# The inverse root of nine normalisations: ScalarE root and VectorE reciprocal, or one power instruction on GpSimd

## The chip, the core and the metric

The kernel runs on one core of a Trainium2 chip. The core's engines that matter here are TensorE (PE, matmuls; PEld is its weight load), VectorE (DVE), ScalarE (ACT), GpSimd (POOL) and SyncE (SP, which only issues loads). The metric is the device time of one execution in microseconds, lower is better; a kernel's figure is the median of its runs.

## What is computed

The program is two transformer-like blocks on one sequence of 256 tokens of width 1024. The first block has two layers, each with a projection, attention beside a Fourier mixer, an output projection and a gated feed-forward part; the second block has a feed-forward part, a mixer, and a second feed-forward part, with gains and shifts computed from a vector `c` by a large product `c_act @ w_ada`. Between these parts stand nine normalisations over the 1024 features:

```python
def layer_norm(x, g, b):                       # normalisations 0 to 4
    mu = jnp.mean(x32, axis=-1, keepdims=True)
    var = jnp.mean(jnp.square(x32 - mu), axis=-1, keepdims=True)
    return ((x32 - mu) * lax.rsqrt(var + LN_EPS) * g + b).astype(x.dtype)

def rmsnorm(x, g):                             # normalisations 5 to 8
    inv = lax.rsqrt(jnp.mean(xf * xf, axis=-1, keepdims=True) + EPS)
    return (xf * inv).astype(x.dtype) * g

def first_block(x, ...):
    h = layer_norm(x, ln_in_g, ln_in_b)                                    # 0
    for l in range(DEPTH):                                                 # DEPTH = 2
        ...
        h = layer_norm(ALPHA * h + mix, ln1_g[l], ln1_b[l])                # 1, 3
        h = layer_norm(ALPHA * h + swiglu(h, w_gu[l], w_down[l]), ...)     # 2, 4

def second_block(x, c, ...):
    u = modulate(rmsnorm(h, norm1_g[l]), mod[:, 0, 0], mod[:, 0, 1])       # 5
    h = h + FFN_RES_WEIGHT * ... * swiglu_2(u, ...)
    u = modulate(rmsnorm(h, norm2_g[l]), ...)                              # 6
    y = mixer(u, ...)
    u = modulate(rmsnorm(h, norm3_g[l]), ...)                              # 7
    ...
    return rmsnorm(h, final_g)                                             # 8
```

## The kernel before

**Layout.** Everything is kept transposed: features lie on the 128 partitions, in eight tiles `k`, and the 256 tokens lie along the row. `state[:, k, 0, :]` is the residual stream and `state[:, k, 1, :]` a scratch beside it. The weights come as 184 chunks of 128x2048 floats, `raw`, in three rotating buffers. Each chunk is split in two parts for an exact product: ACT rounds it to `w_hi` (L670) and DVE takes the rest as `w_lo` (L937). The activations are split in the same way, into `x_hi` (ACT, L696) and `x_lo` (DVE, L979), and every product is three matmuls (L335).

**Order.** There is no scheduler. Each engine has its own program, written out by hand, and the engines meet only at counting semaphores, so an engine that waits holds back all that stands behind it in its own program.

**One normalisation.** Both engines add up values and squares of the eight tiles (L1011, L1003). PE sums them over the partitions with two matmuls against a constant matrix (L388, L391), so that the mean and the mean square of each token stand on all 128 partitions, a tile of 128x256. DVE makes `var` of it: four steps for a layer norm (L946 to L953), one for an RMS norm (L944). The last of these raises `var_ready`. Then come the steps that the change touches:

- ACT waits for `var_ready` and takes the root, `rstd <- var` (L693; L927 for the last normalisation), and raises `std_ready`.
- DVE meanwhile subtracts the mean from tiles 0 and 1 in a layer norm (L960), then waits for `std_ready` and takes the reciprocal, `rstd <- rstd` (L967; L1391 for the last), and raises `rstd_ready`.
- DVE then scales the eight tiles one by one (L973). Each scaled tile goes to ACT for `x_hi`, and back to DVE for `x_lo`, and that raises `x_ready`, for which PE waits before it multiplies the tile. In the last normalisation the scaled tiles (L1394) are the output, which SP stores.

The instruction between `std_ready` and `rstd_ready`:

```python
                dve.wait_ge(std_ready, n + 1)
                nc.vector.reciprocal(rstd[:, :], rstd[:, :]).then_inc(rstd_ready, 1)
                dve.wait_ge(rstd_ready, n + 1)
```

**What PE does meanwhile.** After normalisations 2, 4 and 6 PE has `sum_ada` (L434), 48 small matmuls that add up a third of `c_act @ w_ada`; they wait for none of the normalisation's results. Behind normalisation 4 comes normalisation 5 at once, with nothing between but the squares. After the others PE has nothing until the first `x_lo`.

**GpSimd.** Its program loads two tables and then the 24 tiles of `w_ada` (1.5 MB each) into one buffer. Tile `a` is loaded when DVE has used up tile `a - 1`, which it does in the inner steps of three of the four feed-forward parts, eight tiles in each (L1064, L1067). Before the change it computes nothing.

**Tables of ScalarE.** Before an ACT instruction whose function is not in the active set, the build puts an ACT_TABLE_LOAD. Root, exponential, logarithm, sigmoid and the gate's Silu make it change; squares, copies and additions of a bias do not.

Of the kernel before, what the change touches and what calls it, by code (L numbers as in the profile page):

```python
# [27 lines left out]
ALU = mybir.AluOpType  # L28
ACT = mybir.ActivationFunctionType
AX_X = mybir.AxisListType.X  # L30

P = 128
S = 256
D = 1024
KT = D // P
DEPTH = 2
# [13 lines left out]
ADA_TILES = 9 * D // ADA_COLS  # L50
ADA_STEPS = FT - 3
# [22 lines left out]
def fused_blocks(nc, xT, stream, ada, w_f, layer_params, common_params, consts32, consts16, outT):  # L74
    with ExitStack() as ctx:
        def sb(name, shape, dt=F32):
            return ctx.enter_context(nc.sbuf_tensor(name, shape, dt))

        def sem(name):
            return ctx.enter_context(nc.semaphore(name))  # L80
# [19 lines left out]
        mean = sb("mean", [P, S])  # L100
        var = sb("var", [P, S])
        rstd = sb("rstd", [P, S])
        small = sb("small", [P, 128])
        partial = sb("partial", [P, 2, S])
        partial_last = sb("partial_last", [P, 2, S])
# [93 lines left out]
        mean2_ready = sem("mean2_ready")  # L199
        var_raw = sem("var_raw")  # L200
        var_ready = sem("var_ready")
        std_ready = sem("std_ready")
        rstd_ready = sem("rstd_ready")
        centered = sem("centered")
        scaled = sem("scaled")
# [76 lines left out]
        @block.sync  # L282
        def _(sp):
            for j in range(4):
                sp.dma_start(state[:, 2 * j:2 * j + 2, 0, :],
                             xT[2 * j * P:(2 * j + 2) * P, :].rearrange("(k p) n -> p k n", p=P))\
                  .then_inc(x_landed[j], 16)

            for s in range(SLOTS):
                sp.dma_start(raw[s][:, :], stream[s]).then_inc(raw_landed[s], 16)  # L290
                if s == 1:
                    sp.dma_start(c32[:, 0:ONES_D], consts32[:, 0:ONES_D]).then_inc(consts_landed, 16)
                    sp.dma_start(c32[:, TRI:], consts32[:, TRI:]).then_inc(consts_landed, 16)
            with sp.Fori(1, N_CHUNKS // SLOTS) as t:
                for s in range(SLOTS):

                    sp.wait_ge(lo_ready, 3 * t + (s - 2))
                    sp.dma_start(raw[s][:, :], stream[bass.ds(3 * t + s, 1)].rearrange("a p n -> (a p) n"))\
                      .then_inc(raw_landed[s], 16)
            for c in range(N_CHUNKS // SLOTS * SLOTS, N_CHUNKS):  # L300
                sp.wait_ge(lo_ready, c - 2)
                sp.dma_start(raw[c % SLOTS][:, :], stream[c]).then_inc(raw_landed[c % SLOTS], 16)
            for j in range(4):
                sp.wait_ge(out_ready, 2 * j + 2)
                sp.dma_start(outT[2 * j * P:(2 * j + 2) * P, :].rearrange("(k p) n -> p k n", p=P),
                             state[:, 2 * j:2 * j + 2, 1, :]).then_inc(stored, 16)
            sp.wait_ge(stored, 64)
# [4 lines left out]
        @block.gpsimd  # L312
        def _(pool):
            pool.dma_start(cp[:, :], common_params).then_inc(common_landed, 16)
            pool.wait_ge(raw_landed[1], 16)
            pool.dma_start(c16[:, :], consts16).then_inc(alibi_landed, 16)
            pool.dma_start(ada_raw, ada[0]).then_inc(ada_landed, 16)
            with pool.Fori(1, ADA_TILES) as a:

                pool.wait_ge(ada_step, KT * a)  # L320
                pool.dma_start(ada_raw, ada[bass.ds(a, 1)].rearrange("a p k n -> (a p) k n")).then_inc(ada_landed, 16)

# [339 lines left out]
        def _(act):  # L664
# [7 lines left out]
            def squares(n, j, ready):  # L672
                ready(j)
                nc.scalar.activation(state[:, 2 * j:2 * j + 2, 1, :], state[:, 2 * j:2 * j + 2, 0, :], ACT.Square)\
                    .then_inc(squares_done, 1)
# [11 lines left out]
            def after_residual(m):  # L687
                return lambda j: act.wait_ge(resid_done, 4 * m + (j + 1))

            def norm(n, shift, full):  # L690

                act.wait_ge(var_ready, n + 1)
                nc.scalar.activation(rstd[:, :], var[:, :], ACT.Sqrt).then_inc(std_ready, 1)  # L693
                for k in range(KT):
                    act.wait_ge(scaled, 8 * n + (k + 1))
                    nc.scalar.activation(x_hi[:, k, :], state[:, k, 1, :], ACT.Identity, bias=shift(k))\  # L696
                        .then_inc(x_hi_ready, 1)
                    if full:
                        nc.scalar.activation(state[:, k, 0, :], state[:, k, 1, :], ACT.Identity, bias=shift(k))\
                            .then_inc(full_ready, 1)  # L700
# [45 lines left out]
            split(0, 0, first=True)  # L746
            split(0, 1, first=True)
            norm(0, lambda k: cp[:, LNI_B + k:LNI_B + k + 1], True)

            with act.Fori(0, DEPTH) as l:  # L750
# [69 lines left out]
                for m in range(2):  # L820
# [3 lines left out]
                                         scale=subg).then_inc(mix_a_hi, 1)  # L824
                squares_of_pairs(2 * l + 1, 2 * l, t, O0)
                norm(2 * l + 1, lambda k: lp[:, LN1_B + k:LN1_B + k + 1], True)
                split(t, O0 + 6)
                ffn(t, G0, l)
                for j in range(4):
                    squares(2 * l + 2, j, after_residual(2 * l + 1))  # L830
                split(t, LAYER_CHUNKS + 1)
                norm(2 * l + 2, lambda k: lp[:, LN2_B + k:LN2_B + k + 1], True)


# [88 lines left out]
            ffn(MIX_T, MIX_CHUNKS, 3, final=True)  # L923
            for j in range(4):
                squares(8, j, after_residual(6))
            act.wait_ge(var_ready, 9)
            nc.scalar.activation(rstd[:, :], var[:, :], ACT.Sqrt).then_inc(std_ready, 1)  # L927

# [2 lines left out]
        def _(dve):  # L933
# [6 lines left out]
            def norm_stats(n, eps, rms):  # L940

                dve.wait_ge(stats_done, n + 1)
                if rms:
                    nc.vector.tensor_scalar(var[:, :], STATS[:, S:2 * S], eps, None, ALU.add).then_inc(var_ready, 1)  # L944
                else:
                    nc.vector.tensor_copy(mean[:, :], STATS[:, 0:S]).then_inc(mean_ready, 1)  # L946
                    dve.wait_ge(mean_ready, n + 1)
                    nc.vector.scalar_tensor_tensor(var[:, :], mean[:, :], -1.0, mean[:, :], ALU.mult, ALU.mult)\
                        .then_inc(mean2_ready, 1)
                    dve.wait_ge(mean2_ready, n + 1)  # L950
                    nc.vector.tensor_tensor(var[:, :], STATS[:, S:2 * S], var[:, :], ALU.add).then_inc(var_raw, 1)
                    dve.wait_ge(var_raw, n + 1)
                    nc.vector.tensor_scalar(var[:, :], var[:, :], 0.0, eps, ALU.max, ALU.add).then_inc(var_ready, 1)  # L953

            def norm(n, gain, shift, rms):

                norm_stats(n, RMS_EPS if rms else LN_EPS, rms)

                def center(k):
                    nc.vector.tensor_tensor(state[:, k, 1, :], state[:, k, 0, :], mean[:, :], ALU.subtract)\  # L960
                        .then_inc(centered, 1)

                if not rms:
                    center(0)
                    center(1)
                dve.wait_ge(std_ready, n + 1)
                nc.vector.reciprocal(rstd[:, :], rstd[:, :]).then_inc(rstd_ready, 1)  # L967
                dve.wait_ge(rstd_ready, n + 1)
                for k in range(KT + 1):
                    if k < KT:  # L970
                        if not rms:
                            dve.wait_ge(centered, 8 * n + (k + 1))
                        nc.vector.scalar_tensor_tensor(state[:, k, 1, :], state[:, k, 0 if rms else 1, :], gain(k),  # L973
                                                       rstd[:, :], ALU.mult, ALU.mult).then_inc(scaled, 1)
                        if not rms and k + 2 < KT:
                            center(k + 2)
                    if k >= 1:
                        dve.wait_ge(x_hi_ready, 8 * n + k)
                        nc.vector.scalar_tensor_tensor(x_lo[:, k - 1, :], state[:, k - 1, 1, :], shift(k - 1),  # L979
                                                       x_hi[:, k - 1, :].bitcast(F32), ALU.add, ALU.subtract)\  # L980
                            .then_inc(x_ready, 1)
# [405 lines left out]


            norm_stats(8, RMS_EPS, True)
            dve.wait_ge(std_ready, 9)  # L1390
            nc.vector.reciprocal(rstd[:, :], rstd[:, :]).then_inc(rstd_ready, 1)  # L1391
            dve.wait_ge(rstd_ready, 9)
            for k in range(KT):
                nc.vector.scalar_tensor_tensor(state[:, k, 1, :], state[:, k, 0, :],  # L1394
# [108 lines left out]
```

## Time and profile before

| | |
|---|---|
| median of 3 runs | 1327.15 us (1324.51 to 1329.25) |
| span of the profiled execution | 1327.0 us |
| TensorE matmul busy | 1239.0 us, 93% |
| TensorE weight load busy | 1183.8 us, 89% |
| VectorE busy | 857.9 us, 65% |
| ScalarE busy | 589.8 us, 44% |
| GpSimd busy | 14.1 us, 1% |
| chain that ended last | PE 86%, DVE 6%, ACT 4%, issue 3%, DMA 1% |

The span runs from the first to the last instruction. The busy shares say that PE is the engine to wait for in most of the program. They are averages over stages, though: what matters for a change in the normalisations is where PE stands still, and what it waits for there. The list of waits and the order in time (the timeline) tell that; in both, the bracket or the last columns name the idle time of an engine just before an instruction and the instruction that ended it.

### The profile page before, as it was taken

How to read it: one execution, taken by the hardware profiler on the slowest of the kernel's cores; microseconds unless marked ns; L12 is line 12 of the kernel's file. 1: busy time of each engine (PE TensorE's matmuls, PEld its weight loads, DVE VectorE, ACT ScalarE, POOL GpSimd, SP SyncE). 2: the span in 40 equal slices, each digit the busy share in tenths (PEclk: the TensorE clock that was granted, in tenths of full speed). 3: DMA queues.
4: the chain of work that ended last, by engine and by line, in shares of the span. 5: the costliest groups of instructions: out<-in, count | busy, mean ns of one | idle time of the engine just before them, and what ended most of it. 6: DMA issues, size and time to landing. Idle time of an engine off the chain costs nothing.

```text
span 1327.0 us, 23836 instructions
## 1 busy us (share of the span) xinstructions
PE 1239.0 (93%) x9572; PEld 1183.8 (89%) x9572; DVE 857.9 (65%) x1077; ACT 589.8 (44%) x693; POOL 14.1 (1%) x30
## 2 busy tenths in 40 slices
PE   4998799999999988999994999999999997999996
PEld 3886699999897687999994999999998997999996
DVE  7674756777857657577778467778458567544445
ACT  5543444333444335344335433444487534444432
POOL 0000000000000000000000000000000000000000
PEclk9999899999899898999996999998999998999998
DMA  7510256677442113577770467773432553455540
GB/s 285 201 64 32 96 191 231 270 276 282 175 149 86 63 64 129 188 284 276 271 275 33 174 224 283 283 274 140 154 133 96 191 188 130 160 190 190 184 164 32
DMA packets 34093, 235.95 MB, mean 178 GB/s; under 512 B 3600, under 2 KB 7200, under 8 KB 7408
## 3 DMA queue, kind: packets, MB, share of 16 engines
q1 hardware_dynamic: 28960, 196.10, 40.2%
q0 software_dynamic: 3584, 38.22, 7.8%
q8 instruction: 45, 0.74, 0.2%
q10 hardware_dynamic: 1488, 0.76, 0.2%
q14 instruction: 16, 0.13, 0.0%
HBM read 234.02 MB, written 1.05 MB: 177 GB/s over the span
## 4 chain that ended last, share of the span: by engine, by line
PE 86%; DVE 6%; ACT 4%; issue 3%; DMA 1%; SPq 0%; DVEq 0%; ACTq 0%
PE bank L335 78%; PE bank L454 2%; ACT w_hi L670 2%; PE bank L434 1%; PE bank L474 1%; DVE rstd L967 1%; PE bank L486 1%; DMA raw<-stream 1%; DVE partial L1011 1%; PE bank L466 1%; DVE w_lo L937 1%; DVE state L960 1%; PE bank L450 0%; DVE state L973 0%; DVE x_lo L979 0%
## 5 line engine op out<-in xcount | busy, mean ns | idle before, releaser
L937 DVE TENSOR_TENSOR w_lo<-raw,w_hi 128x2048 fp32r<-128x2048 f32 x184 | 421.4, 2290 | 240.9 <-ACT w_hi L670 238.3
L335 PE MATMUL bank<-x_hi,w_hi 128*128 128x256 f32 x1888 | 541.3, 287 | 25.3 <-DVE x_lo L979 24.3
L335 PE MATMUL bank<-x_lo,w_hi 128*128 128x256 f32 x1888 | 537.9, 285 | 0.0
L335 PE MATMUL bank<-x_hi,w_lo 128*128 128x256 f32 x1888 | 537.5, 285 | 0.0
L670 ACT ACTIVATE w_hi<-raw 128x2048 fp32r<-128x2048 f32 x184 | 350.2, 1906 | 156.9 <-PE bank L335 154.3
L335 PEld LDWEIGHTS bank<-x_hi,w_hi 128*128 128x128 f32 x1888 | 366.0, 194 | 32.0 <-DVE x_lo L979 15.8
L335 PEld LDWEIGHTS bank<-x_lo,w_hi 128*128 128x128 f32 x1888 | 366.2, 194 | 0.0
L335 PEld LDWEIGHTS bank<-x_hi,w_lo 128*128 128x128 f32 x1888 | 366.0, 194 | 0.0
L335 PE MATMUL bank<-hid_hi,w_lo 128*128 128x256 f32 x704 | 197.9, 281 | 0.0
L335 PE MATMUL bank<-hid_hi,w_hi 128*128 128x256 f32 x704 | 197.3, 280 | 0.0
L335 PE MATMUL bank<-hid_lo,w_hi 128*128 128x256 f32 x704 | 195.8, 278 | 0.0
L335 PEld LDWEIGHTS bank<-hid_lo,w_hi 128*128 128x128 f32 x704 | 132.5, 188 | 0.0
L335 PEld LDWEIGHTS bank<-hid_hi,w_hi 128*128 128x128 f32 x704 | 132.5, 188 | 0.0
L335 PEld LDWEIGHTS bank<-hid_hi,w_lo 128*128 128x128 f32 x704 | 132.1, 188 | 0.0
L1067 DVE SCALAR_TENSOR_TENSOR work<-work,c_act 128x384 f32 x168 | 104.0, 619 | 5.9
L711 ACT ACTIVATE hid_hi<-work 128x512 fp32r<-128x512 f32 x44 | 27.8, 631 | 159.0 <-PE bank L335 137.2
L707 ACT ACTIVATE work<-bank 128x512 f32<-128x512 f32 x44 | 26.3, 598 | 138.9 <-PE bank L335 138.9
L1055 DVE TENSOR_TENSOR hid_lo<-work,hid_hi 128x512 fp32r<-128x512 f32 x44 | 30.4, 691 | 84.0 <-ACT hid_hi L711 84.0
L335 PE MATMUL bank<-w_hi,x_hi 128*128 128x256 f32 x160 | 49.9, 312 | 8.4 <-DVE x_lo L979 8.4
L335 PE MATMUL bank<-mix_hi,w_hi 128*128 128x256 f32 x192 | 54.5, 284 | 0.0
L335 PE MATMUL bank<-mix_lo,w_hi 128*128 128x256 f32 x192 | 54.3, 283 | 0.0
L335 PE MATMUL bank<-mix_hi,w_lo 128*128 128x256 f32 x192 | 54.3, 283 | 0.0
(158 smaller groups left out, 1175.7 us busy)
## 6 DMA issues: line engine op xcount, KB each, us to landing
raw<-stream SPq DMA_DIRECT2D x184, 1024.0 KB, 4.8
work<-ada POOLq DMA_DIRECT2D x24, 1536.0 KB, 7.1
state<-xT SPq DMA_DIRECT2D x4, 256.0 KB, 3.6
outT<-state SPq DMA_DIRECT2D x4, 256.0 KB, 2.2
c<-consts SPq DMA_DIRECT2D x1, 960.0 KB, 9.9
wf<-w_f ACTq DMA_DIRECT2D x2, 256.0 KB, 3.1
c<-consts POOLq DMA_DIRECT2D x1, 384.0 KB, 5.6
lp<-layer_params ACTq DMA_DIRECT2D x2, 83.5 KB, 2.5
```

The costliest lines, as they stand in the source:

```text
L335: last = nc.tensor.matmul(out, stationary, moving, start=start and i == 0, stop=stop and i == 2, skip_group_check=True)
L434: last = nc.tensor.matmul(B[6][:, q:q + 1], ada_acc[:, q * P:(q + 1) * P], ones[:, 0:1], start=True, stop=True, skip_group_check=True)
L454: last = nc.tensor.matmul(bank[:, m * S:(m + 1) * S], qT[r:r + HD, h // 2, m * P:(m + 1) * P], kT[r:r + HD, h // 2, :], start=False, stop= ...
L466: last = nc.tensor.transpose(B[6][:, kk * S + m * P:kk * S + (m + 1) * P], a_s[:, m, kk * P:(kk + 1) * P], ident)
L474: last = nc.tensor.matmul(B[4 + m][:, h * VD:(h + 1) * VD], aT_s[:, kk, m * P:(m + 1) * P], v_s[:, kk, h * VD:(h + 1) * VD], start=kk == 0 ...
L486: last = nc.tensor.matmul(B[7][:, :], u_s[:, m, g * P:(g + 1) * P], dft_s[:, m, :], start=m == 0, stop=m == 1)
L670: nc.scalar.activation(w_hi[j % SLOTS][:, :], raw[j % SLOTS][:, :], ACT.Copy).then_inc(hi_ready, 1)
L707: nc.scalar.activation(gate_act, B[0][:, :], ACT.Silu).then_inc(silu_done, 1)
L711: nc.scalar.activation(out[:, :, :].rearrange("p k n -> p (k n)"), hidden, ACT.Copy)\
L937: nc.vector.tensor_tensor(w_lo[j % SLOTS][:, :], raw[j % SLOTS][:, :], w_hi[j % SLOTS][:, :].bitcast(F32), ALU.subtract).then_inc(lo_ready, 1)
L1055: nc.vector.tensor_tensor(lo[:, :, :].rearrange("p k n -> p (k n)"), hidden, hi[:, :, :].rearrange("p k n -> p (k n)").bitcast(F32), ALU.s ...
L1067: nc.vector.scalar_tensor_tensor(acc, ada_raw[:, k, :], c_act[:, k:k + 1], acc, ALU.mult, ALU.add).then_inc(ada_step, 1)
```

## The change

The root on ACT and the reciprocal on DVE go, and GpSimd computes `var ** -0.5` in one `tensor_tensor` instruction with the operation `pow`; its second operand is a column of -0.5, broadcast over the 256 tokens. DVE waits for `rstd_ready` as before, which GpSimd now raises. Since a `tensor_tensor` has to stand at its place in GpSimd's program, the single loop over the tiles of `w_ada` is written out by stage. The root of the attention heads (`head_std`, on ACT, with its reciprocal on DVE) stays as it is.

```diff
+        neg_half = sb("neg_half", [P, 1])
...
         @block.gpsimd
-            with pool.Fori(1, ADA_TILES) as a:
+            nc.gpsimd.memset(neg_half[:, :], -0.5).then_inc(neg_half_ready, 1)
+            pool.wait_ge(neg_half_ready, 1)
+            def inverse_root(n):
+                pool.wait_ge(var_ready, n + 1)
+                nc.gpsimd.tensor_tensor(rstd[:, :], var[:, :], neg_half[:, :].broadcast_to([P, S]), ALU.pow).then_inc(rstd_ready, 1)
+            def next_ada_tile(a):
                 pool.wait_ge(ada_step, KT * a)
                 pool.dma_start(ada_raw, ada[bass.ds(a, 1)].rearrange("a p k n -> (a p) k n")).then_inc(ada_landed, 16)
+            inverse_root(0)
+            with pool.Fori(0, DEPTH) as l:
+                inverse_root(2 * l + 1)
+                with pool.Fori(0, ADA_STEPS) as i:
+                    next_ada_tile(ADA_STEPS * l + i + 1)
+                inverse_root(2 * l + 2)
+            inverse_root(5)
+            with pool.Fori(ADA_STEPS * DEPTH + 1, ADA_TILES) as a:
+                next_ada_tile(a)
+            for n in (6, 7, 8):
+                inverse_root(n)
...
         @block.scalar
             def norm(n, shift, full):
-                act.wait_ge(var_ready, n + 1)
-                nc.scalar.activation(rstd[:, :], var[:, :], ACT.Sqrt).then_inc(std_ready, 1)
                 for k in range(KT):
...
-            act.wait_ge(var_ready, 9)
-            nc.scalar.activation(rstd[:, :], var[:, :], ACT.Sqrt).then_inc(std_ready, 1)
...
         @block.vector
             def norm(n, gain, shift, rms):
-                dve.wait_ge(std_ready, n + 1)
-                nc.vector.reciprocal(rstd[:, :], rstd[:, :]).then_inc(rstd_ready, 1)
                 dve.wait_ge(rstd_ready, n + 1)
...
             norm_stats(8, RMS_EPS, True)
-            dve.wait_ge(std_ready, 9)
-            nc.vector.reciprocal(rstd[:, :], rstd[:, :]).then_inc(rstd_ready, 1)
             dve.wait_ge(rstd_ready, 9)
```

ScalarE's program from the end of a layer's second normalisation to the first gate of the next feed-forward part (normalisation 5 stands in it), before the change:

```order
233 L674 ACTIVATE state<-state 128x2x256 x4
234 L693 ACTIVATE rstd<-var 128x256
235 L696 ACTIVATE x_hi<-state,mods 128x256 x8
236 L670 ACTIVATE w_hi<-raw 128x2048
237 L707 ACT_TABLE_LOAD
238 L707 ACTIVATE work<-bank 128x512
```

and with it:

```order
227 L695 ACTIVATE state<-state 128x2x256 x4
228 L715 ACTIVATE x_hi<-state,mods 128x256 x8
229 L691 ACTIVATE w_hi<-raw 128x2048
230 L726 ACTIVATE work<-bank 128x512
231 L691 ACTIVATE w_hi<-raw 128x2048 x2
```

The root is gone, and so is the table load ahead of the gate, since the set of the gate's function is still active from the layer before.

VectorE's program in normalisations 2 and 4, from the variance to the first scaled tile, before the change:

```order
L953 TENSOR_SCALAR var<-var 128x256
L960 TENSOR_TENSOR state<-state,mean 128x256 x2
L967 RECIPROCAL rstd<-rstd 128x256
L972 ISA
L973 SCALAR_TENSOR_TENSOR state<-state,lp,rstd 128x256
```

and with it:

```order
L970 TENSOR_SCALAR var<-var 128x256
L977 TENSOR_TENSOR state<-state,mean 128x256 x2
L987 ISA
L988 SCALAR_TENSOR_TENSOR state<-state,lp,rstd 128x256
L977 TENSOR_TENSOR state<-state,mean 128x256
```

Between the subtraction and the first scaled tile DVE has no instruction left; it waits there for GpSimd.

GpSimd's program with the change, from the first tile of `w_ada` to the end of the loop over the layers:

```order
L318 DMA work<-ada 128x3072
L319 MEMSET neg_half 128x1
L325 ISA
L325 TENSOR_TENSOR rstd<-var,neg_half 128x256 [waits var_ready,neg_half_ready]
L333 UNCONDITIONAL_BRANCH
L333 ISA
L325 TENSOR_TENSOR rstd<-var,neg_half 128x256 [waits var_ready]
L335 UNCONDITIONAL_BRANCH
L335 ISA
L330 ISA [waits ada_step]
L330 DMA work<-ada 128x3072
```

The power now stands ahead of the eight loads of a layer, and a second one behind them; before, the loads stood in one loop with nothing else.

## Rows read from the trace of the kernel before

**Rows 1.** The page: the span, and PE's busy time, share, instructions.

```profile
span 1327.0 us, 23836 instructions
PE 1239.0 (93%) x9572; PEld 1183.8 (89%) x9572; DVE 857.9 (65%) x1077; ACT 589.8 (44%) x693; POOL 14.1 (1%) x30
```

**Rows 2.** Waits of PE: who waited for whom, us in total, times, longest.

```profile
PE bank L335 <- DVE x_lo L979: 32.7, 5, 8.4
PE bank L388 <- DVE partial L1011: 29.6, 6, 10.7
```

**Rows 3.** Timeline of ACT and DVE, normalisation 1: start, us, instruction [idle before].

```profile
153.84 0.29 DVE L953 TENSOR_SCALAR var<-var 128x256 f32<-128x256 f32 x1
154.05 0.75 DVE L960 TENSOR_TENSOR state<-state,mean 128x256 f32<-128x256 f32 x2
154.16 0.42 ACT L693 ACTIVATE rstd<-var 128x256 f32<-128x256 f32 x1 [4.54 <-DVE var L953]
154.72 1.74 DVE L967 RECIPROCAL rstd<-rstd 128x256 f32<-128x256 f32 x1
156.60 0.48 DVE L973 SCALAR_TENSOR_TENSOR state<-state,lp,rstd 128x256 f32<-128x256 f32 x1
```

**Rows 4.** The same of normalisation 5, an RMS norm.

```profile
719.97 0.42 DVE L944 TENSOR_SCALAR var<-bank 128x256 f32<-128x256 f32 x1 [1.83 <-PE bank L391]
720.42 0.42 ACT L693 ACTIVATE rstd<-var 128x256 f32<-128x256 f32 x1 [3.59 <-DVE var L944]
720.87 1.75 DVE L967 RECIPROCAL rstd<-rstd 128x256 f32<-128x256 f32 x1 [0.48 <-ACT rstd L693]
722.66 0.88 DVE L973 SCALAR_TENSOR_TENSOR state<-state,gains,rstd 128x256 f32<-128x256 f32 x2
```

**Rows 5.** Timeline of PE and DVE at normalisation 2.

```profile
354.83 10.24 PE L434 MATMUL bank<-c,work 128*128 128x1 f32 x48
360.98 0.48 DVE L979 SCALAR_TENSOR_TENSOR x_lo<-state,lp,x_hi 128x256 fp32r<-128x256 f32 x1
```

**Rows 6.** The same at normalisation 6.

```profile
918.38 9.20 PE L434 MATMUL bank<-c,work 128*128 128x1 f32 x48
925.02 0.48 DVE L979 SCALAR_TENSOR_TENSOR x_lo<-state,mods,x_hi 128x256 fp32r<-128x256 f32 x1 [0.18 <-ACT x_hi L696]
```

**Rows 7.** Groups of instructions: line, shapes, count | busy us, mean ns | idle before, releaser.

```profile
L937 DVE TENSOR_TENSOR w_lo<-raw,w_hi 128x2048 fp32r<-128x2048 f32 x184 | 421.4, 2290 | 240.9 <-ACT w_hi L670 238.3 <-issue 2.7
...
L967 DVE RECIPROCAL rstd<-rstd 128x256 f32<-128x256 f32 x8 | 14.0, 1747 | 1.4 <-ACT rstd L693 1.4
...
L693 ACT ACT_TABLE_LOAD x5 | 6.4, 1283 | 0.1
```

**Rows 8.** PE after normalisation 3: stretch, us, PE, PEld, DVE, ACT, POOL, granted clock, DMA.

```profile
504.00:508.00 4.00, 3.91 (x18) 3.91 (x19) 4.00 (x12) 3.19 (x8) 0.00 (x0) 0.50 0.02 4
```

**Rows 9.** Timeline of ACT: table loads ahead of a gate, a root, the last root.

```profile
730.93 1.28 ACT L707 ACT_TABLE_LOAD   x1
737.18 0.60 ACT L707 ACTIVATE work<-bank 128x512 f32<-128x512 f32 x1 [4.97 <-PE bank L335]
...
1117.69 1.28 ACT L693 ACT_TABLE_LOAD   x1
1120.70 0.42 ACT L693 ACTIVATE rstd<-var 128x256 f32<-128x256 f32 x1 [1.72 <-DVE var L944]
...
1317.11 1.28 ACT L927 ACT_TABLE_LOAD   x1
1318.90 0.42 ACT L927 ACTIVATE rstd<-var 128x256 f32<-128x256 f32 x1 [0.51 <-DVE var L944]
```

**Rows 10.** Timeline of POOL: a memset, the eighth load of layer 0, the last load.

```profile
0.38 0.10 POOL L1497 MEMSET const-float32-0.0<- 128x1 f32 x1 [0.38 <-issue]
...
337.04 0.53 POOL L321 DMA_DIRECT2D work<-ada  x1 [16.65 <-DVE work L1067]
...
885.92 0.53 POOL L321 DMA_DIRECT2D work<-ada  x1 [16.65 <-DVE work L1067]
```

More of the change, by code:

```diff
@@ L201, in fused_blocks @@
         var_ready = sem("var_ready")
-        std_ready = sem("std_ready")
+        neg_half_ready = sem("neg_half_ready")
         rstd_ready = sem("rstd_ready")
```

## The prediction

> **What bounds the kernel now.** I read the page first [rows 1]: PE is busy 93% of the 1327.0 us, so a change in the normalisations can only touch what is left, and there only where PE stands still. The waits of PE say where that is [rows 2]. Five times PE waits for the first `x_lo` of a normalisation, 32.7 us in all: in time order these are normalisations 0, 1, 3, 5 and 7. Six times it waits for the sums that lead to a normalisation, 29.6 us, the longest 10.7 us being the one of normalisation 5, which cannot begin before 4 has ended. So 4 is on the path too, through 5. Normalisation 8 is the end of the program. That makes seven of nine on the path. In the other two, 2 and 6, PE has `sum_ada` to do [rows 5, 6].
>
> Next I read the timeline of one layer norm [rows 3] and one RMS norm [rows 4], from the end of the variance to the first scaled tile. In the layer norm the variance ends at 153.84 + 0.29 = 154.13 and the first scaled tile starts at 156.60: **2.47 us**, made of a hand-over, the root of 0.42, another hand-over and the reciprocal of 1.74. In the RMS norm it is 719.97 + 0.42 = 720.39 to 722.66: **2.27 us**. Hand-overs between engines are short: ACT starts 0.03 after the variance [rows 3, 4], DVE 0.03 after the root [rows 4], and the first scaled tile starts 0.04 to 0.14 after the reciprocal ends.
>
> **Part 1, what goes.** On the path the seven normalisations give up 4 x 2.47 (0, 1, 3, 4) + 3 x 2.27 (5, 7, 8) = 9.9 + 6.8 = **16.7 us**. With the roots go seven table loads of 1.28 us: five ahead of a root in a normalisation [rows 7], the one ahead of the last root and the one ahead of the gate behind normalisation 5 [rows 9]. I cost them at nothing. After each, ACT sat idle anyway: 1.72 us after the one of normalisation 7, 4.97 after the gate's, 0.51 after the last [rows 9]. That idle time is what hides them; if it were gone, each would be worth up to 1.28. The reciprocal's 1.74 us on DVE is free for nothing else, since DVE's next instruction waits for the same result.
>
> The Trainium skill (ScalarE: Activation LUTs, "Table sets: the hidden batching unit") says to order activations by set, since each switch costs about 2.7 us. By it the seven loads would be worth 19 us. The trace has 1.28 us for one, not 2.7, and idle time behind each one that I looked at, so by the trace the sum has zero here.
>
> **Part 2, what comes.** One power over 128x256 on GpSimd, with its hand-overs: call the power P, and the two hand-overs 0.1 us. Everything hangs on P, and the trace of before has no row for it. GpSimd computes nothing there but memsets of one column, 0.10 us each [rows 10]. I bound it by rows of other engines:
>
> - Below: the cheapest step over a 128x256 tile in these rows is one pass on DVE or ACT, 0.42 us [rows 4]. A power is no less work than a pass, so P is at least 0.4.
> - In between: the reciprocal, 1.75 us [rows 7], is the only function in these rows that is worked out on its engine and not taken from a table. One pass of DVE over 256 columns costs, above its fixed part, 256 x (2290 - 420) / (2048 - 256) ns = 0.27 us, and the fixed part is 0.42 - 0.27 = 0.15 [rows 4, 7]. The reciprocal is then (1.75 - 0.15) / 0.27 = 6 passes long.
> - Above: a power is a logarithm, a product and an exponential. If the logarithm and the exponential are each one and a half reciprocals, 9 passes, and the product and the taking apart of the number are two more, that is 20 passes: 0.15 + 20 x 0.27 = **5.5 us**. Half as many give 2.9 us, twice as many 11 us. That GpSimd does a pass at DVE's pace is an assumption of this estimate.
>
> I take 5.4 us. It is nearer to the reciprocal's row than to the pass's, because a power cannot be cheaper arithmetic than a reciprocal unless a table does it, and no row shows such a table outside ACT.
>
> The Trainium skill (GPSIMD Engine Reference, "Elementwise — side-by-side cycle accounting") speaks against the change: it has a two-input add of 2048 columns at 4497 ns on GpSimd against 2293 on DVE. The trace agrees for DVE, 2290 [rows 7], and shows nothing for GpSimd. By the page, a reciprocal's work at 1.96 times DVE's time would be 3.4 us and the kernel 1335; a power no dearer than an add would be about 0.6 us (an estimate from the page's 2.6 cycles per element at 1.2 GHz) and the kernel 1315.
>
> **Part 3, the cover of 2 and 6.** In 2 PE is in `sum_ada` until 354.83 + 10.24 = 365.07, and the first `x_lo` is there at 360.98 + 0.48 = 361.46 [rows 5]: 3.6 us to spare. In 6 the same is 927.58 against 925.50 [rows 6]: 2.1 us to spare. So they cost nothing until P + 0.1 is above 2.47 + 3.6 = 6.1 in one and 2.27 + 2.1 = 4.4 in the other, and everything beyond.
>
> **Part 4, GpSimd's queue.** Behind a power that waits stand the loads of `w_ada`, and behind the loads the next power. The last load of layer 0 is issued at 337.04, 24 us ahead of the first `x_lo` of normalisation 2 at 360.98, and the last of all at 885.92, 39 us ahead of that of 6 at 925.02 [rows 5, 6, 10]; the variances come some 4 us before these `x_lo`, so some 20 and 35 us stay. The loads that stand behind powers 1, 3 and 5 are not due before the inner steps of the feed-forward part, tens of microseconds later. Cost nothing. The memset of -0.5 runs while DVE has yet to make a variance: nothing. DVE's two subtractions in a layer norm run beside the power; they end 0.67 us after the variance, so they hold back nothing once P is above 0.6 [rows 3].
>
> **PE's clock.** After normalisation 3 the granted clock is 0.50 for the first 4 us, the level of 1.2 GHz [rows 8], PE having waited before it. It is down already, so a longer wait takes no further level; I add nothing.
>
> **The sum.** Time = 1327.0 + 7 x (P + 0.1) - 16.7 + (what is uncovered in 2 and 6). With P = 5.4: 7 x 5.5 = 38.5, less 16.7 is +21.8; nothing in 2, 5.5 - 4.4 = 1.1 in 6. Together +22.9, so **1350 us**. The profiled span, 1327.0, is 0.15 below the median of 1327.15, so I use it as it is. The point at which the change is neither gain nor loss is P = 16.7 / 7 - 0.1 = 2.3 us.
>
> **The rivals.**
>
> A. *The power is cheap*, P below 1.7 us. For it: in these rows a function of a table costs one pass, 0.42 us, and GpSimd might have something like it. Against it: the reciprocal alone is six passes. At the lower end a layer norm is held by its subtractions (0.67 + 0.1) and an RMS norm by the pass (0.42 + 0.1): 4 x 0.77 + 3 x 0.52 = 4.6, less 16.7 is -12.1, so 1315. At P = 1.7 it is 12.6 - 16.7 = -4.1, so 1323. This is the rival on the other side; it decides at P = 2.3.
>
> B. *The power is as dear as what it replaces*, P from 1.7 to 2.8: 1323 to 1331. For it: 2.3 us is only a third above the one reciprocal row.
>
> C. *The power is very dear*, P above 11 us, where each element is done by many short steps that don't overlap. At 11: 7 x 11.1 - 16.7 = 61.0, with 5.0 in 2 and 6.7 in 6 it is +73, so 1400. At 12 it is 1409, at 20: +124 + 14 + 16, so 1481. For it: nothing in these rows limits P from above. Against it: nothing either, but it would be 6 times and more the reciprocal.
>
> D. *The seven table loads do count* where I saw ACT idle, by the skill's rule on sets: at most 7 x 1.28 = 9 us off the forecast, 1341. Against it stand the idle times in rows 9. It stays inside the forecast's range.
>
> E. *The change doesn't do what it says*: a power is held back in GpSimd's queue by the loads ahead of it. Against it stand the 20 and 35 us of room of part 4; a normalisation that lost this room would wait for a load's issue of 0.53 us, within a microsecond of the forecast.
>
> **How the numbers follow.** Forecast, P from 2.9 to 11: chance 0.46, own range 1331 to 1400. D: 0.02. E: 0.01. A: 0.24. B: 0.13. C: 0.14. The predicted time is that of the forecast with P = 5.4. The range takes in A down to its bound, 1315, and C up to P = 12, 1409; what is left out is nearly all of C, some 0.13. A measurement of this kernel can tell 0.3%, 4 us, from no change. A is faster by more than that, B is within it, the rest is slower: 0.24, 0.13, 0.63.
>
> **What the profile would show.** A group `rstd<-var` on POOL, nine instructions of 128x256, whose mean time is P: this one row decides most. The distance from the end of the variance to the first scaled tile, 2.47 and 2.27 before, is P + 0.1 in all nine. PE's five waits for `x_lo` grow by 5 x (P + 0.1) less 12.0, from 32.7 to about 48, and the longest wait for the sums from 10.7 to about 14. At 2 the first product still starts when `sum_ada` ends; at 6 about 1 us later. The number of table loads on ACT falls by seven with no change in the time of anything else. The loads of `w_ada` stay at their distance of 17 us. The prediction is wrong if P is below 2.3 us, or if GpSimd's hand-over, which no row shows, is not 0.1 but a microsecond: each microsecond on either counts seven times.

## The result: 349 us slower

The changed kernel takes a median of 1675.53 us (1674.67 to 1678.23, 4 runs) against 1326.16 us (1324.51 to 1329.25, 4 runs) before. The ratio is **1.2635**, 95% interval 1.2613 to 1.2658. The span of its profiled execution is 1674.1 us, 347.1 more than the 1327.0 of [rows 1]; between the medians it is 349.4. (A time lies 1.6 to 2 us above the span of its own execution, 1676.0 above 1674.1 here, so spans are compared with spans below.) The time is outside the range that was forecast, 1315 to 1409.

The page of the changed kernel: span, busy times, the busy slices of POOL and the granted clock, and the two groups of instructions that matter (line, shapes, count | busy us, mean ns | idle before, releaser).

```profile
span 1674.1 us, 23823 instructions
PE 1238.3 (74%) x9562; PEld 1185.6 (71%) x9572; DVE 845.1 (50%) x1068; ACT 577.3 (34%) x677; POOL 385.2 (23%) x40
...
POOL 6400360000540036000056700004500008100018
PEclk7799869999679985999975599997699995899995
...
L356 PE MATMUL bank<-x_hi,w_hi 128*128 128x256 f32 x1888 | 541.5, 287 | 181.2 <-DVE x_lo L994 180.2
L325 POOL TENSOR_TENSOR rstd<-var,neg_half 128x256 f32<-128x256 f32 x9 | 370.7, 41185 | 756.4 <-DVE var L961 442.1
```

PE does the same work as in [rows 1], 1238.3 us against 1239.0; all the new time is standing still. The second group is the answer to the open question: one power over 128x256 takes **41.2 us**, nine times 370.7 us.

The timeline of normalisation 1 and of 5 in the changed kernel (start, us, instruction, idle before), to be set beside [rows 3] and [rows 4]:

```profile
194.57 0.29 DVE L970 TENSOR_SCALAR var<-var 128x256 f32<-128x256 f32 x1
194.78 1.17 DVE L977 TENSOR_TENSOR state<-state,mean 128x256 f32<-128x256 f32 x2
194.94 41.24 POOL L325 TENSOR_TENSOR rstd<-var,neg_half 128x256 f32<-128x256 f32 x1 [135.93 <-DVE var L970]
236.32 0.48 DVE L988 SCALAR_TENSOR_TENSOR state<-state,lp,rstd 128x256 f32<-128x256 f32 x1 [40.37 <-POOL rstd L325]
...
912.09 41.12 POOL L325 TENSOR_TENSOR rstd<-var,neg_half 128x256 f32<-128x256 f32 x1 [14.46 <-DVE var L961]
953.24 0.88 DVE L988 SCALAR_TENSOR_TENSOR state<-state,gains,rstd 128x256 f32<-128x256 f32 x2 [41.23 <-POOL rstd L325]
```

The way from the variance to the first scaled tile was 2.47 us and is 236.32 - 194.86 = 41.46. GpSimd starts 0.08 after the variance, and DVE starts 0.03 to 0.14 after GpSimd has ended: the hand-overs are as short as between the other engines. The wait of 40.37 us on DVE is the power and nothing else.

Behind normalisations 2 and 6 the cover of `sum_ada` is now far too short. PE's timeline there, the answer to [rows 5] and [rows 6]:

```profile
434.57 10.24 PE L455 MATMUL bank<-c,work 128*128 128x1 f32 x48
480.74 0.58 PE L356 MATMUL bank<-w_hi,x_hi 128*128 128x256 f32 x1 [35.92 <-DVE x_lo L994]
...
1149.13 9.09 PE L455 MATMUL bank<-c,work 128*128 128x1 f32 x48
1195.40 0.55 PE L356 MATMUL bank<-w_hi,x_hi 128*128 128x256 f32 x1 [37.18 <-DVE x_lo L994]
```

And PE's waits as a whole (who waited for whom, us in total, times, longest), the answer to [rows 2]:

```profile
PE bank L356 <- DVE x_lo L994: 300.8, 7, 47.5
PE bank L409 <- DVE partial L1026: 68.4, 6, 49.5
```

Seven waits for `x_lo` instead of five, since 2 and 6 have joined, 300.8 us instead of 32.7; and the longest wait for sums, normalisation 5's, is 49.5 instead of 10.7. Together PE waits 306.9 us longer in these two rows. Normalisation 8, behind which PE has nothing left, adds 41.3 - 2.3 = 39 us at the end, which makes 346 of the 347.

The prediction's own sum, with 41.2 in place of 5.4 for P, is 7 x 41.3 = 289.1, less 16.7, plus 41.3 - 6.1 = 35.2 for normalisation 2 and 41.3 - 4.4 = 36.9 for 6: +344.5, a span of 1671.5. The trace has 1674.1. So the build of the sum holds to 2.6 us, or to 4.9 by the medians, and one price in it was wrong. The trace says where the 2.6 us are. PE's waits and the end grew by 345.9 us, 1.4 more than the sum. The stretches of work between them grew by 1.2: 1.7 more from the first product behind normalisation 0 to the wait at 1, 2.0 less from 2 to 3, 1.1 more from 7 to 8, and 0.5 in all the rest. These stretches hold the same instructions, and the granted clock in them differs; the part on the clock further down has the rows.

### The profile page after: what moved, and what is told of

It reads as the page before. It is cut to its first block, busy times and chain, and to the rows that moved or that the text cites. A ratio compares the mean times of both kernels' runs of the same rounds, so it can differ in the third digit from the quotient of the medians.

```text
span 1674.1 us, 23823 instructions
## 1 busy us (share of the span) xinstructions
PE 1238.3 (74%) x9562; PEld 1185.6 (71%) x9572; DVE 845.1 (50%) x1068; ACT 577.3 (34%) x677; POOL 385.2 (23%) x40
## 4 chain that ended last, share of the span: by engine, by line
issue 40%; PE 40%; POOL 12%; ACT 3%; POOLq 2%; DVE 2%; DMA 1%; SPq 0%; DVEq 0%; ACTq 0%
PE bank L356 39%; POOL rstd L325 12%; POOLq L75 2%; ACT w_hi L691 1%; DVE work L1082 1%; DMA raw<-stream 1%; DVE w_lo L954 0%; ACT L895 0%; ACT L889 0%; ACT L891 0%; ACT work L889 0%; DVE state L1407 0%; ACT work L887 0%; ACT work L895 0%; ACT work L891 0%
## 5 line engine op out<-in xcount | busy, mean ns | idle before, releaser
L325 POOL TENSOR_TENSOR rstd<-var,neg_half 128x256 f32<-128x256 f32 x9 | 370.7, 41185 | 756.4 <-DVE var L961 442.1
L330 POOL DMA_DIRECT2D work<-ada x23 | 12.4, 538 | 515.4 <-DVE work L1082 515.4
L356 PEld LDWEIGHTS bank<-w_hi,x_hi 128*128 128x128 f32 x160 | 35.1, 220 | 122.3 <-DVE x_lo L994 85.1
L988 DVE SCALAR_TENSOR_TENSOR state<-state,lp,rstd 128x256 f32<-128x256 f32 x32 | 15.3, 479 | 161.5 <-POOL rstd L325 161.5
L715 ACT ACTIVATE x_hi<-state,lp 128x256 fp32r<-128x256 f32 x32 | 16.2, 505 | 188.9 <-DVE state L988 188.9
```

The source lines that it names most:

```text
L325: nc.gpsimd.tensor_tensor(rstd[:, :], var[:, :], neg_half[:, :].broadcast_to([P, S]), ALU.pow).then_inc(rstd_ready, 1)
L356: last = nc.tensor.matmul(out, stationary, moving, start=start and i == 0, stop=stop and i == 2, skip_group_check=True)
```

## The experiments

Each kernel ran beside the kernel before on the same chip, and ratios are to that.

### e1: what a power costs by itself

```diff
 (the kernel before, GpSimd, behind its last load)
+            pool.wait_ge(var_ready, 8)
+            nc.gpsimd.memset(value, 3.7); nc.gpsimd.memset(exponent, -0.5)
+            test(2, ALU.add, S, exponent)
+            test(3, ALU.mult, S, column.broadcast_to([P, S]))
+            test(4, ALU.pow, S, column.broadcast_to([P, S]))
+            test(5, ALU.pow, S, exponent)
+            test(6, ALU.pow, 128, exponent[:, 0:128])
+            test(7, ALU.pow, 64, exponent[:, 0:64])
+            test(8, ALU.pow, 2, exponent[:, 0:2])
+            test(9, ALU.pow, S, value)
```

What was expected:

> The kernel before, with a row of instructions in GpSimd's program that nobody waits for, on free tiles, once the variance of normalisation 7 is there: add of two full tiles of 128x256, product with a broadcast column, power with a broadcast column of -0.5, power with a full tile of -0.5, powers of 128, 64 and 2 columns, power with a full tile of 3.7. Theory 1 (the power has a price per column, about 161 ns, whatever the operand): add and product under 1 us, the three powers of 256 columns 41 us each, 20.6 for 128, 10.3 for 64, under 0.6 for 2. Theory 2 (a fixed price for each power): 41 us for each. Theory 3 (the broadcast operand is what is slow): with a full tile under 5 us. Theory 4 (any two-input step on GpSimd is slow): add and product tens of us as well. Time: 1326 as before if GpSimd's work disturbs nothing; if VectorE's two-input steps are held up by it in the 150 us that the probes last, 5 to 20 us more.

Measured: ratio 1.0008 (0.9997 to 1.0019), no change in time. POOL's timeline of e1, an instruction at a time, in the order of the diff without the product and the power of two columns:

```profile
1121.51 0.72 POOL L333 TENSOR_TENSOR work<-work 128x256 f32<-128x256 f32 x1
1122.77 41.14 POOL L333 TENSOR_TENSOR work<-work 128x256 f32<-128x256 f32 x1
1163.90 43.13 POOL L333 TENSOR_TENSOR work<-work 128x256 f32<-128x256 f32 x1
1207.01 20.77 POOL L333 TENSOR_TENSOR work<-work 128x128 f32<-128x128 f32 x1
1227.76 11.55 POOL L333 TENSOR_TENSOR work<-work 128x64 f32<-128x64 f32 x1
1240.36 41.12 POOL L333 TENSOR_TENSOR work<-work 128x256 f32<-128x256 f32 x1
```

The group of the power of two columns:

```profile
L333 POOL TENSOR_TENSOR work<-work 128x2 f32<-128x2 f32 x1 | 1.1, 1103 | 0.0
```

An add is 0.72 us, and between its end and the first power lie 0.54 us, in which the product is. So two-input steps on GpSimd are not slow as such, and theory 4 falls. A power of 256 columns is 41.1 us, with the broadcast column and with a full tile of 3.7 alike, and 43.1 with the full tile of -0.5: it is not the broadcast (theory 3). 128 columns are 20.8 us, and 256 less 128 is 20.4 us for 128 columns: **0.16 us a column**, with next to nothing fixed (theory 2 falls, theory 1 stands). 64 columns took 11.6 us instead of 10.3, and two took 1.1 instead of under 0.6; why these and the 43.1 are a microsecond or two above the line was not looked into, and neither was what GpSimd does inside a power. The 159 us of powers beside the last feed-forward part did not disturb its time: VectorE's split of a chunk (L937 in [rows 7]) takes 2.29 us there with them and without.

### e2: everything as in the change, but a product

```diff
-            nc.gpsimd.memset(neg_half[:, :], -0.5).then_inc(neg_half_ready, 1)
+            nc.gpsimd.memset(neg_half[:, :], 0.002).then_inc(neg_half_ready, 1)
-                nc.gpsimd.tensor_tensor(rstd[:, :], var[:, :], neg_half[:, :].broadcast_to([P, S]), ALU.pow)...
+                nc.gpsimd.tensor_tensor(rstd[:, :], var[:, :], neg_half[:, :].broadcast_to([P, S]), ALU.mult)...
```

What was expected:

> The changed kernel with a product in place of the power (operand 0.002, so the numbers are not the reference's); order, waits, engines and loads as in the changed kernel. Theory 1 (all of the loss is the power's own duration): the sum with P = 0.7 gives 4 x 0.8 + 3 x 0.8 - 16.7 = -11, so 1315. Rival (hand-over to and from GpSimd, or the place in its queue, costs): each microsecond of it counts seven times, so 1327 or more.

Measured: 1316.97 us, ratio **0.9925** (0.9906 to 0.9943), span 1314.4. POOL's group in e2:

```profile
L325 POOL TENSOR_TENSOR rstd<-var,neg_half 128x256 f32<-128x256 f32 x9 | 6.0, 665 | 760.7 <-DVE var L961 443.0 <-DVE var L970 317.6
```

PE's waits in e2, beside [rows 2]:

```profile
PE bank L356 <- DVE x_lo L994: 27.2, 6, 7.6
PE bank L409 <- DVE partial L1026: 23.9, 6, 9.9
```

With an instruction of 0.67 us at the same place, behind the same waits, the kernel would be 10 us faster than before, by the medians. So GpSimd's hand-overs and its queue cost nothing that shows, and the whole loss is the power's duration. It also says about what a cheap inverse root of 256 columns in this place could bring: some 0.75%.

The sixth wait for `x_lo` is a surprise. It is that of normalisation 2, which the prediction has as covered. The first product behind it in e2:

```profile
361.21 0.57 PE L356 MATMUL bank<-w_hi,x_hi 128*128 128x256 f32 x1 [1.39 <-DVE x_lo L994]
```

The 48 matmuls of `sum_ada` took 10.24 us in [rows 5], at a granted clock of 0.50, and take 7.25 here (352.58 to 359.83), at 0.73. So the 3.6 us of cover were a figure of that one execution and not of the kernel.

### e3: half of the columns

```diff
-                nc.gpsimd.tensor_tensor(rstd[:, :], var[:, :], ...broadcast_to([P, S]), ALU.pow)
+                nc.gpsimd.tensor_tensor(rstd[:, 0:P], var[:, 0:P], ...broadcast_to([P, P]), ALU.pow)
+                nc.scalar.activation(rstd[:, P:S], var[:, P:S], ACT.Sqrt).then_inc(std_ready, 1)
+                nc.vector.reciprocal(rstd[:, P:S], rstd[:, P:S]).then_inc(rstd_right, 1)
```

What was expected:

> GpSimd takes the power of columns 0 to 127 only; columns 128 to 255 go the old way, root on ScalarE and reciprocal on VectorE, beside it. Theory 1: P = 20.7, so 1327 + 7 x 20.8 - 16.7 + 14.7 + 16.4 = 1487. Theory 2 (fixed price): 1675 as with the change.

Measured: 1491.72 us, ratio 1.1237 (1.1218 to 1.1256), span 1489.7. POOL's group in e3:

```profile
L327 POOL TENSOR_TENSOR rstd<-var,neg_half 128x128 f32<-128x128 f32 x9 | 187.1, 20784 | 755.9 <-DVE var L967 441.7 <-DVE var L976 314.2
```

Half the columns, half the duration, and the span of the whole kernel is 2.7 us above the expected 1487 (4.7 by the medians, 164.7 more than before where 160 were expected). The sum, seven on the path and two partly covered, holds at a second value of P. The cover of normalisation 6 came out, with a wait of 16.23 us where 16.4 were worked out. That of 2 did not: `sum_ada` took 7.28 us there, at a clock of 0.72, as in e2, and PE waited 19.04 us where 14.7 were worked out. From the start of `sum_ada` to the first product that is 16.1 us more than before, so 1.4 us of the miss are here.

### e4: the table loads by themselves

```diff
-                nc.scalar.activation(rstd[:, :], var[:, :], ACT.Sqrt).then_inc(std_ready, 1)
+                nc.scalar.activation(rstd[:, :], var[:, :], ACT.Copy).then_inc(std_ready, 1)
```

What was expected:

> The kernel before with a copy in place of the nine roots on ScalarE (so the inverse variance stands where the inverse root belongs, and the numbers are not the reference's): same instructions and durations, but the seven table loads are gone. Theory of the prediction (they lie in ScalarE's idle time): 1326, within 2 us. Rival (they are on the path): 7 x 1.28 = 9 us less, 1317.

Measured: ratio 1.0000 (0.9987 to 1.0013). The copies in the place of the roots, from the groups of e4:

```profile
L693 ACT ACTIVATE rstd<-var 128x256 f32<-128x256 f32 x8 | 3.3, 417 | 30.2 <-DVE var L953 20.9 <-DVE var L944 9.3
```

Their duration is that of the roots, and ACT's idle time ahead of eight of them is 30.2 us; in the kernel before it was 17.0 + 6.7 = 23.7 in the waits for these variances. The 6.5 us between are the five table loads ahead of these roots (6.4 us in [rows 7]), turned into idle time. The rival's 9 us would be 0.7%, and the interval excludes it. The Trainium skill (ScalarE: Activation LUTs, "Table sets: the hidden batching unit") counts about 2.7 us for each switch of set; here seven switches together cost nothing that shows.

### e5 and e6: two columns instead of 256

If the power costs 0.16 us a column, the columns have to go. The variance stands 128 times over on the partitions; laid with the tokens on the partitions it is 128x2.

```diff
 (PE, stats)
-                nc.tensor.matmul(out, ones_over_d, partial[:, a, :]..., start=True, stop=False)
+                nc.tensor.matmul(TOK[:, 2 * a + m:2 * a + m + 1], part[:, a, m * P:(m + 1) * P], ones_over_d[:, 0:1], ...)
 (PE, behind stats, or inside sum_ada)
+                nc.tensor.matmul(out[:, m * P:(m + 1) * P], column[:, m:m + 1].broadcast_to([P, P]), ident, ...)
 (e5, GpSimd)
+                nc.gpsimd.tensor_tensor(rstd_s[:, :], var_s[:, :], neg_half[:, :], ALU.pow)
 (e6, ScalarE and VectorE)
+                nc.scalar.activation(rstd_s[:, :], var_s[:, :], ACT.Sqrt)
+                nc.vector.reciprocal(rstd_s[:, :], rstd_s[:, :])
```

What was expected of e5, and then of e6:

> The change's instruction at the size that its price per column asks for. PE sums squares and values with the tokens on the partitions (the sums as stationary operand, a column of 1/1024 moving), so that mean and variance are 128x2 instead of 128x256; GpSimd takes the power of 2 columns; PE spreads mean and inverse root over the partitions again with two products against the identity; after normalisations 2, 4 and 6 that happens inside sum_ada. Theory 1 (price per column): the power is 0.6 to 1.1 us; the four small steps of a layer norm's variance are 0.2 each instead of 0.45; the spreading costs 1 us on PE. A layer norm from the end of PE's sums to the first scaled tile: 2.5 instead of 4.1, an RMS norm 2.0 instead of 2.7, so 4 x 1.6 + 3 x 0.7 = 8 us less on the path, about 1319. Theory 2 (fixed price per power): 1675. Rival to the gain: the way through PE costs what the small tiles save, 1327 or more.

> As e5_two_columns_pow, but with the root on ScalarE and the reciprocal on VectorE, both on 128x2: about 0.2 each and two hand-overs, 0.45 us where GpSimd's power has 0.6 to 1.1. Expected 1 to 4 us below e5, about 1316. If the two are the same, then the engine does not matter at this size; if both are at 1327 or above, the way through PE eats the gain.

Measured: e5 1327.69 us, ratio 1.0007 (0.9994 to 1.0020); e6 1327.52 us, ratio 1.0001 (0.9990 to 1.0011). Both expectations missed: no gain at all, and no difference between the two that could be told. First the power, POOL's group in e5:

```profile
L330 POOL TENSOR_TENSOR rstd_s<-var_s,neg_half 128x2 f32<-128x2 f32 x9 | 6.3, 699 | 767.2 <-DVE var_s L992 450.5 <-DVE var_s L1001 316.7
```

At two columns the change's instruction is harmless, 0.70 us. Then the timeline of normalisation 1 in e6, ACT, DVE and PE:

```profile
152.01 0.15 DVE L977 COPY mean_s<-bank 128x2 f32<-128x2 f32 x1
...
152.59 0.17 DVE L984 TENSOR_SCALAR var_s<-var_s 128x2 f32<-128x2 f32 x1
152.79 0.20 ACT L724 ACTIVATE rstd_s<-var_s 128x2 f32<-128x2 f32 x1 [3.62 <-DVE var_s L984]
153.03 0.17 DVE L995 RECIPROCAL rstd_s<-rstd_s 128x2 f32<-128x2 f32 x1 [0.27 <-ACT rstd_s L724]
153.25 1.22 PE L401 MATMUL bank<-c,rstd_s 128*128 128x128 f32 x4
...
154.61 0.48 DVE L1005 SCALAR_TENSOR_TENSOR state<-state,lp,bank 128x256 f32<-128x256 f32 x1 [0.38 <-PE bank L401]
```

From the mean's copy to the first scaled tile it is 154.61 - 152.01 = 2.60 us. In the kernel before the same way starts at

```profile
152.47 0.42 DVE L946 COPY mean<-bank 128x256 f32<-128x256 f32 x1
```

and ends at 156.60 [rows 3], 4.1 us. So on the path the small form gains 1.5 us, near the expected 1.6. The loss is in the places where PE had been covered. PE's timeline of e6 at normalisation 6:

```profile
917.83 1.22 PE L401 MATMUL bank<-c,rstd_s 128*128 128x128 f32 x4 [3.00 <-DVE rstd_s L995]
918.84 9.38 PE L457 MATMUL bank<-c,work 128*128 128x1 f32 x44
928.09 0.56 PE L340 MATMUL bank<-w_hi,x_hi 128*128 128x256 f32 x1
```

The spreading stands in PE's program inside `sum_ada`, four matmuls in, and there PE waits 3.00 us for an inverse root that DVE makes only behind the split of a weight chunk, and then works 1.22 us that it did not work before. Before, `sum_ada` started at 918.38 and ended at 927.58 [rows 6] with nothing in it. The first product behind normalisation 5 in e6, and the first products behind 5 and 6 in the kernel before:

```profile
719.67 0.55 PE L340 MATMUL bank<-x_hi,w_hi 128*128 128x256 f32 x1 [1.73 <-DVE x_lo L1011]
...
724.35 0.55 PE L335 MATMUL bank<-x_hi,w_hi 128*128 128x256 f32 x1 [4.42 <-DVE x_lo L979]
...
927.43 0.56 PE L335 MATMUL bank<-w_hi,x_hi 128*128 128x256 f32 x1
```

Behind 5 e6 is 4.7 us ahead; behind 6, at 928.09, it is 0.7 us late. The distance between the two has grown from 203.1 to 208.4 us, and the lead is gone. `sum_ada` still starts 4.1 us ahead in e6, at 914.24 instead of 918.38, so 4.8 of these 5.3 us are lost inside it.

### e7: the small form only where PE waits anyway

```diff
 (as e6 in normalisations 1, 3, 5, 7 and 8; 0, 2, 4 and 6 and sum_ada as before)
```

What was expected:

> The form of e6 (statistics of 128x2, root on ScalarE, reciprocal on VectorE, spread by PE) only in normalisations 1, 3, 5, 7 and 8, which PE waits for; 0, 2, 4 and 6 stay as in the kernel before, so nothing stands inside sum_ada. In e6 the first product behind normalisation 1 came 2.0 us earlier than before, but behind 2 it came 0.7 us later and behind 6 (4.7 us ahead at 5) 0.7 us later. Theory (the gain of e6 was lost in sum_ada, where the spreads of 1.2 us are PE's own time and wait for VectorE): 2 x 2.0 + 2 x 1.4 + 1.3 = 8 us less than before, 1319, and the first product behind 2 and 6 not later than before. Rival (the earlier start is lost again elsewhere, in the stretch at half clock behind each normalisation): 1326, as e6.

Measured: 1320.53 us (1319.42 to 1325.06, 6 runs), ratio **0.9947** (0.9931 to 0.9963): by the ratio 7 us faster than before, by the medians 8, where 8 were expected. Normalisation 5 in e7, in the order of time, beside [rows 4], and the first product behind 6:

```profile
718.80 0.16 DVE L977 TENSOR_SCALAR small<-bank 128x2 f32<-128x2 f32 x1 [1.62 <-PE bank L404]
718.99 0.20 ACT L722 ACTIVATE small<-small 128x2 f32<-128x2 f32 x1 [3.13 <-DVE small L977]
719.23 0.17 DVE L1000 RECIPROCAL small<-small 128x2 f32<-128x2 f32 x1 [0.27 <-ACT small L722]
719.45 1.22 PE L411 MATMUL bank<-c,small 128*128 128x128 f32 x4 [0.69 <-DVE small L1000]
720.71 0.88 DVE L1017 SCALAR_TENSOR_TENSOR state<-state,gains,bank 128x256 f32<-128x256 f32 x2 [1.31 <-PE bank L411]
722.40 0.55 PE L340 MATMUL bank<-x_hi,w_hi 128*128 128x256 f32 x1 [1.73 <-DVE x_lo L1023]
...
925.47 0.56 PE L340 MATMUL bank<-w_hi,x_hi 128*128 128x256 f32 x1
```

From the variance's start to the first scaled tile 1.91 us instead of 722.66 - 719.97 = 2.69. And from the first product behind 5 to that behind 6 it is 925.47 - 722.40 = 203.07 us, as in the kernel before, and not the 208.4 of e6: the cover is left alone and the lead is kept. The profiled execution took 1325.06 us and is late already before normalisation 1, so only distances within it are used here. From the matmuls of the sums to the first product, normalisations 1 and 3 are 1.55 us shorter each, 5 is 1.0 and 7 is 0.8, and from the sums of 8 to the end it is 1.2: 6.1 us of the gain stand where they were sought. e7 also takes the small form out of 0 and 4, so it does not show by itself that all of e6's loss was in `sum_ada`; for normalisation 6 the trace of e6 shows it. This kernel beats both: it is what the change was after, without the power.

## Why the prediction was wrong

- **The price of the power: wrong, and it is nearly the whole error.** The step that failed is "Above" in part 2, "a power is a logarithm, a product and an exponential ... 20 passes", together with the assumption that stands at its end, that GpSimd does a pass at DVE's pace. It gave 5.5 us, with 11 as its upper end; e1 has 41.1, that is 41.1 / 0.27 = 152 of DVE's passes, seven to eight times the 20. GpSimd's pace is a small part of that: a product is 0.67 us on GpSimd in e2, where DVE takes 0.42 for a tile of this size, 1.6 times as long. The rest, a factor of nearly five, is the count of passes, or the way in which GpSimd does a power; no run looks inside one, so that cause stays open. The 20 was a count of arithmetic that no row bore out, and the range was cut at P = 12 although the text said of rival C that nothing in the rows limits P from above. With a price without an upper bound, multiplied by seven to nine, an upper end of 1409 had no ground.
- **The rivals.** C, "the power is very dear", came true with a chance of 0.14. A and B, on the other side, are ruled out by the same row. D is too: its table loads were worth 0 within 0.13% (e4). In part 1 the prediction sets the 1.28 us of a load's row against a figure of 2.7; in the Trainium skill (ScalarE: Activation LUTs, "What ACT_TABLE_LOAD costs") that figure is for a whole switch, and the load by itself has the 1.28 of the trace. The zero rests on e4. E did not happen: the loads of `w_ada` kept their distance, and e2, with the same queue, was faster than before.
- **What goes, 16.7 us: right, to about a microsecond.** e2 puts a cheap instruction in the place: 7 x (0.67 + 0.1) - 16.7 = -11.3 was to be expected. The medians have -10.0, and the spans -12.6, but 2.5 of these come from normalisations 2 and 6, where `sum_ada` ran faster. From the sums to the first product, or to the end, the seven on the path gave 10.0. What is missing is in the layer norms: their two subtractions take 1.17 us beside the product instead of 0.75, so the first scaled tile starts 1.02 us after the variance and not 0.77; and in normalisation 0 the variance itself came half a microsecond later behind its sums than before.
- **Hand-overs of 0.1 us: right**, 0.08 and 0.03 to 0.14 in the changed kernel.
- **The cover of 2 and 6: right.** With P = 41.2 the prediction's formula gives 35.2 and 36.9 us; PE's waits there are 35.92 and 37.18. Five waits for `x_lo` were to grow to 32.7 + 5 x 41.3 - 12.0 = 227; with these two that makes 300, and the row has 300.8. The longest wait for sums was to be 10.7 + 41.3 - 2.5 = 49.5, and is 49.5. That normalisation 2 fits so well is in part luck: `sum_ada` took 10.24 us in this execution as in [rows 5], and three microseconds less in e2 and e3.
- **PE's clock: a small miss, in the mechanism too.** I added nothing for it, since "it is down already". That was read off normalisation 3, where it is so: nothing was added there. It is not so behind 0 and 7. Windows of the kernel before behind 0 and 7, then of the changed kernel behind 7 (stretch, us, busy times, granted clock, DMA):

```profile
22.00:26.00 4.00, 4.00 (x21) 4.00 (x22) 4.00 (x12) 3.20 (x8) 0.00 (x0) 1.00 0.86 356
...
1124.60:1128.00 3.40, 3.37 (x17) 3.40 (x18) 3.40 (x10) 2.03 (x4) 0.00 (x0) 0.54 0.00 0
...
1431.70:1435.70 4.00, 3.98 (x19) 4.00 (x20) 4.00 (x11) 2.54 (x5) 0.00 (x0) 0.50 0.00 0
1435.70:1437.70 2.00, 2.00 (x13) 2.00 (x13) 1.10 (x3) 1.74 (x2) 0.00 (x0) 0.65 0.00 0
```

  Behind 0 PE had waited 8.4 us before, and the clock stayed at 1.00; with the change it waited 47.5 us, and the next 4 us were at 0.50. Behind 7 the level of 1.2 GHz lasts for most of 6 us instead of 3.4, in which PE does half the work: about 1 us at this one restart, and the stretch from 7 to 8 is 1.1 us longer. From 0 to 1 it is 1.7 us longer. From 2 to 3 it is 2.0 us shorter: over the first 100 us behind 2 the mean granted clock was 0.94 before and is 0.96 with the change, and 2% of 100 us is these 2 us. Before, it fell between 435 and 455 us, in the middle of the work; why there, no run here shows.

## What to carry to other kernels

An operation for which the trace has no row has no upper bound, and if it stands on the path seven times it has to be measured by itself first: eight instructions on an engine that idles, on free tiles, told the price here to the percent and cost the kernel nothing. Before a function is moved to another engine, look at how many columns it is computed on: this one was computed on 256 columns with the same values on all partitions, and two columns were enough. And a step that is shortened by a detour over the engine that bounds the kernel gains only where that engine would stand still; where it is covered, the detour is its own time (e6 against e7).

## What the runs showed of the hardware

- A power on GpSimd costs 0.16 us per column of 128 partitions, 41.1 us for 256 (41.1 and 43.1 in the three forms of e1); a product of the same tile costs 0.67 and an add 0.72, about a sixtieth. The Trainium skill (GPSIMD Engine Reference, "Elementwise — side-by-side cycle accounting") gives 2.6 cycles per element for a two-input add, from which the prediction estimated 0.6 us for an add of this size; e1 is near it, with 0.72.
- VectorE's two subtractions in a layer norm take 1.17 us beside the start of the power, against 0.75 in [rows 3]. It costs nothing here, since they are done long before the power is. In e2, where the product is done first, they hold back the first scaled tile by 0.25 us in a layer norm.
- A power of two columns takes 0.70 us as a mean of nine (e5). The root on ScalarE, the reciprocal on VectorE and the hand-over between them take 0.44 (e6, 152.76 to 153.20). Seven times the difference is 2 us, which the times of e5 and e6 cannot tell.
